# A hybrid decoder's mixer put into one order of steps for all engines: attention projections in pieces between the steps of the inversion

## The reference, cut to what matters

```python
for l in range(2):
    x = x + 0.5 * swiglu(rms_norm(x, ffn1_norm[l]), ...)
    h = rms_norm(x, mix_norm[l])
    dq, dk, dv, iq, ik, iw, gq, gk, gv, gz, ga, gb, mq = split_columns(h @ w_in[l])
    # A, 6 heads x 64: q and k normed per head; scores of the lightning indexer,
    #   sum_h iw_h * relu(iq_h . ik), 8 heads x 32; the 128 best keys of each query are kept,
    #   then softmax attention with a relative bias over them
    # B, 6 heads x 64: gated delta rule in chunks of 64 on silu(conv4(gq, gk, gv));
    #   needs the inverse of a unit lower triangle for each chunk; rms_norm, times silu(gz)
    # C, 4 heads x 64: attention of mq over 256 memory tokens, keys and values rms_norm(mem) @ w_mem_kv
    x = x + concat(A, B, C) @ w_out[l]
    x = x + 0.5 * swiglu(rms_norm(x, ffn2_norm[l]), ...)
```

## Time and profile before

| | |
|---|---|
| median of 3 runs | 2494.97 us (2494.83 to 2496.26) |
| the profiled execution's own time | 2497.04 us |
| its span | 2495.3 us |
| PE, DVE, ACT, POOL busy | 2359.1, 1121.6, 747.8, 455.5 us |
| mean granted clock of PE | 0.946 |

### The profile page before, as it was taken

One profiled execution on the slowest core, in us unless ns is written; L12 is line 12 of the kernel. 1 busy time (PEld: TensorE's weight loads), 2 busy tenths in 40 slices (PEclk: granted clock), 3 DMA queues, 4 the chain that ended last, 5 costly groups with the idle time before them and its releaser, 6 DMA issues.

```text
span 2495.3 us, 33780 instructions
## 1 busy us (share of the span) xinstructions
PE 2359.1 (95%) x14076; PEld 1882.7 (75%) x14076; DVE 1121.6 (45%) x1504; ACT 747.8 (30%) x983; POOL 455.5 (18%) x352
## 2 busy tenths in 40 slices
PE   7999999998889899999999999999879988999999
PEld 5888886776666778888878888868756767788887
DVE  4444333788543244343343343357874433443322
ACT  3222223433442132222232222244243321322221
POOL 4111011222432211110111110112224322111100
PEclk9999999999887799999999999998988968999999
DMA  4222221211000122222222222212210002222222
GB/s 150 101 95 90 93 94 67 102 68 68 28 2 1 68 81 88 101 99 93 95 85 101 101 84 99 100 41 99 85 62 17 2 1 84 85 86 99 97 93 80
DMA packets 28044, 192.32 MB, mean 77 GB/s; under 512 B 3104, under 2 KB 3232, under 8 KB 8992
## 3 DMA queue, kind: packets, MB, share of 16 engines
q1 hardware_dynamic: 27648, 189.80, 22.0%
q10 hardware_dynamic: 288, 0.94, 0.1%
HBM read 188.64 MB, written 2.10 MB: 76 GB/s over the span
## 4 chain that ended last, share of the span: by engine, by line
PE 84%; DVE 7%; issue 5%; POOL 2%; ACT 2%; DMA 0%; SPq 0%; POOLq 0%; ACTq 0%
PE psum L653 24%; PE psum L654 23%; PE psum L655 23%; PE psum L991 2%; PE psum L979 2%; PE psum L779 1%; DVE wl L1366 1%; PE psum L762 1%; DVE wrk L1449 1%; PE psum L965 1%; PE psum L858 1%; DVE gqT L1467 1%; POOL BT L584 1%; DVE m L1447 1%; PE psum L903 1%
## 5 line engine op out<-in xcount | busy, mean ns | idle before, releaser
L653 PE MATMUL psum<-XH,wh 128*128 128x512 f32 x1920 | 768.1, 400 | 53.0 <-DVE XL L1378 18.2
L654 PE MATMUL psum<-XL,wh 128*128 128x512 f32 x1920 | 754.5, 393 | 0.0
L655 PE MATMUL psum<-XH,wl 128*128 128x512 f32 x1920 | 753.9, 393 | 0.0
L653 PEld LDWEIGHTS psum<-XH,wh 128*128 128x128 f32 x1920 | 364.2, 190 | 146.7 <-issue 38.3
L654 PEld LDWEIGHTS psum<-XL,wh 128*128 128x128 f32 x1920 | 364.0, 190 | 81.5 <-issue 5.9
L655 PEld LDWEIGHTS psum<-XH,wl 128*128 128x128 f32 x1920 | 363.4, 189 | 79.0
L1066 ACT ACTIVATE wh<-raw 128x2048 fp32r<-128x2048 f32 x86 | 164.5, 1913 | 545.7 <-PE psum L655 545.4
L1366 DVE TENSOR_TENSOR wl<-raw,wh 128x2048 fp32r<-128x2048 f32 (+1 forms) x86 | 184.3, 2143 | 269.8 <-ACT wh L1066 269.8
L653 PE MATMUL psum<-HH,wh 128*128 128x512 f32 x704 | 278.1, 395 | 0.0
L655 PE MATMUL psum<-HH,wl 128*128 128x512 f32 x704 | 278.1, 395 | 0.0
L654 PE MATMUL psum<-HL,wh 128*128 128x512 f32 x704 | 278.1, 395 | 0.0
(11 more groups left out here) (241 smaller groups left out, 2429.0 us busy)
## 6 DMA issues: line engine op xcount, KB each, us to landing
raw<-weights SPq DMA_DIRECT2D x144, 1024.0 KB, 4.9
raw<-weights SPq DMA_DIRECT2D x32, 896.0 KB, 4.6
strips<-strip_table SPq DMA_DIRECT2D x2, 1536.0 KB, 6.6
xT<-xt SPq DMA_DIRECT2D x4, 512.0 KB, 9.3
memT<-memt SPq DMA_DIRECT2D x2, 1024.0 KB, 5.1
out<-xT SPq DMA_DIRECT2D x8, 256.0 KB, 6.0
cst<-masks ACTq DMA_DIRECT2D x1, 835.5 KB, 8.3
colsb<-cols ACTq DMA_DIRECT2D x1, 85.0 KB, 5.4
```

Source lines behind the costliest of these rows:

```text
L653: pe.matmul(out_ap, a_hi, b_hi, start=first, stop=False)
L654: pe.matmul(out_ap, a_hi, b_lo, start=False, stop=False)
L655: return pe.matmul(out_ap, a_lo, b_hi, start=False, stop=last)
```

## The change

All engines now walk one list, `MIX_ORDER`, which `_order()` writes. The units and groups stand in another order: iq, ik, sm, mk, mv, the twelve g groups, then dq, dk, va, mq, vb. The last five are cut into pieces of the eight slices and laid behind the steps of the set-up and of the inversion (`pull`); all are through behind the step y of level 4 of the second half. The 44 slots come after `u`: four behind u, three behind each r1, two behind each r2.

Selection is dealt out in 15 rounds over the g groups and 33 over the inversion. The index scores are six batches of four heads; each head keeps its own 32 rows of iqT and of ikT (which holds the key four times over), and writes its own psum bank. `ikz` is gone. The first tap of conv (`tap`) is done by ACT instead of DVE, the copies of transposed gv by ACT instead of DVE. LO_DVE is 1, so POOL splits seven of eight slices. POOL makes BT two levels ahead. The memory tokens are loaded at the start of the mixer, in SP's queue ahead of unit 2, and squared and split between the first groups. SBUF is laid out anew so that XH and XL stay whole through the inversion.

```diff
-MIX_SRC = (["iq", (O_DQ, 256), "small", (O_DQ + 256, 256), (O_DQ + 512, 256), (O_DV, 256), (O_DV + 256, 128)]
-           + [(O_MQ, 256)] + ["mk", "mv"] + [(O_G + 256 * i, 256) for i in range(6)]
+MIX_SRC = (["iq", "small", "mk", "mv"] + [(O_G + 256 * i, 256) for i in range(6)]
+           + [(O_DQ, 256), (O_DQ + 256, 256), (O_DQ + 512, 256), (O_DV, 256), (O_MQ, 256), (O_DV + 256, 128)]
...
+def _order():
+    order = []
+    rounds = [(b, r) for b in range(1, NB) for r in range(TOPK // 8)]
+    def sel(n):
+        for _ in range(min(n, len(rounds))):
+            order.append(("sel",) + rounds.pop(0))
+    def mm(name, c):
+        order.append(("mm", GROUP_AT[name, c], 0, KD))
+    def ev(name, c):
+        order.append(("ev", GROUP_AT[name, c]))
+    def norm(kind, *which):
+        for w in which:
+            order.append((kind, NORMS.index(w)))
+    def put(*names):
+        for n in names:
+            order.append(n if isinstance(n, tuple) else (n,))
+    mm("iq", 0)
+    put("ss", "rr")
+    ev("iq", 0)
+    put("mem1")
+    mm("iq", 1)
+    ev("iq", 1)
+    put("mem2")
+    mm("ik", 0)
+    put("mem3")
+    ev("ik", 0)
+    put("mem4")
+    mm("sm", None)
+    ev("sm", None)
+    put("mem5")
+    mm("mk", 0)
+    put("smt")
+    ev("mk", 0)
+    norm("sq", ("mk", 0))
+    put(("idx", 0), "gate1")
+    mm("mk", 1)
+    ev("mk", 1)
+    norm("sq", ("mk", 1))
+    put(("idx", 1), "gate2")
+    mm("mv", 0)
+    ev("mv", 0)
+    put("gate3", ("idx", 2))
+    mm("mv", 1)
+    ev("mv", 1)
+    put("gate4", ("idx", 3))
+    gates = {0: "gate5", 1: "gate6", 2: "gate7"}
+    pairs = [[("gq", 0), ("gq", 1)], [("gq", 2), ("gk", 0)], [("gk", 1), ("gk", 2)]]
+    for n in range(12):
+        name, c = ("gq", "gk", "gv", "gz")[n // 3], n % 3
+        mm(name, c)
+        if n == 3:
+            norm("hs", ("mk", 0), ("mk", 1))
+            norm("rs", ("mk", 0), ("mk", 1))
+        ev(name, c)
+        if n < 9:
+            put(("tap", n), ("conv", n))
+        if n < 2:
+            put(("idx", 4 + n))
+        if n in gates:
+            put(gates[n])
+        if n == 4:
+            norm("ap", ("mk", 0), ("mk", 1))
+        if n == 7:
+            put("silu_qk")
+            norm("sq", *pairs[0])
+        if n in (8, 9, 10):
+            norm("hs", *pairs[n - 8])
+            norm("rs", *pairs[n - 8])
+            norm("ap", *pairs[n - 8])
+            if n < 10:
+                norm("sq", *pairs[n - 7])
+        if n >= 2:
+            sel(1 if n < 7 else 2)
+    fill = []
+    for name, c in ([("dq", c) for c in range(3)] + [("dk", c) for c in range(3)] + [("va", b) for b in range(NB)]
+                    + [("mq", c) for c in range(2)] + [("vb", b) for b in range(NB)]):
+        cost = {"va": 0.36, "vb": 0.33}.get(name, 0.68)
+        fill += [(name, c, k, cost) for k in range(KD)]
+    later = []
+    def pull(target):
+        now = [x for t, x in later if t <= 0]
+        later[:] = [(t - 1, x) for t, x in later if t > 0]
+        for x in now:
+            order.append(x)
+        while fill and target > 0:
+            name, c, k, cost = fill.pop(0)
+            gi = GROUP_AT[name, c]
+            if order[-1][0:2] == ("mm", gi):
+                order[-1] = ("mm", gi, order[-1][2], k + 1)
+            else:
+                order.append(("mm", gi, k, k + 1))
+            target -= cost
+            if k == KD - 1:
+                order.append(("ev", gi))
+                if (name, c) in NORMS:
+                    nj = NORMS.index((name, c))
+                    later.extend([(0, ("sq", nj)), (1, ("hs", nj)), (1, ("rs", nj)), (2, ("ap", nj))])
+    put("silu_vz")
+    pull(5.4)
+    put(("vt", 0), ("vt", 1))
+    while order[-1][0] != "mm":
+        pull(1.3)
+    put(("vt", 2), ("vt", 3))
+    left = sum(x[3] for x in fill) - 9 * 0.7
+    for i, step in enumerate(INVERSION):
+        order.append(step)
+        pull(0.68 if i < 9 else left / 25)
+        if i >= 9:
+            sel(2 if step[0] == "x" else 1)
+    while fill or later:
+        pull(5.4)
+    put("ready")
+    slots = iter(range(N_SLOTS))
+    for step in RECURRENCE:
+        order.append(step)
+        for _ in range({"r1": 3, "r2": 2, "u": 4}.get(step[0], 0)):
+            n = next(slots, None)
+            if n is not None:
+                order.append(("att", n))
+        sel(1 if step[0] in ("u", "r1", "r2") else 0)
+    for n in slots:
+        order.append(("att", n))
+    assert not rounds
+    return order
...
                     for v in range(U_MIX, U_MIX + MIX_UNITS):
+                        if v == U_MIX + 2:
+                            sp.wait_ge(S["dn_done"], KD * (3 * L + 1))
+                            sp.dma_start(memT[:, :, :], memt).then_inc(S["mem_in"], 16)
...
-                        if v == U_MIX + 4:
-                            sp.wait_ge(S["sc_done"], 24)
-                            sp.wait_ge(S["acc_done"], 24)
-                            sp.dma_start(memT[:, :, :], memt).then_inc(S["mem_in"], 16)
...
-LO_DVE = 3
+LO_DVE = 1
...
+                        elif kind in ("kq", "y"):
+                            if kind == "kq":
+                                ahead = [(at_[0], 0)] if at_[0] < 2 else [(at_[0] - 2, 1)]
+                            else:
+                                g, j = at_
+                                ahead = [(b, j + 2) for b in (2 * g, 2 * g + 1) if j + 2 < LEVELS]
+                                ahead += [(b + 2, j + 2 - LEVELS) for b in (0, 1) if g == 0 and j + 2 >= LEVELS]
+                            for b, j in ahead:
...
+                    for step in MIX_ORDER:
+                        if step[0] == "ev":
+                            split_rest(step[1])
+                        elif step[0] == "att":
+                            combine(step[1] + 2)
+                        else:
+                            gdn(*step)
...
+                    def index_scores(batch):
+                        b, h0 = 1 + batch // 2, 4 * (batch % 2)
+                        wait_copied(GROUP_AT["ik", 0])
+                        if batch == 0:
+                            pe.wait_ge(S["mem_r"], 1)
+                        for i in range(4):
+                            n = 4 * batch + i
+                            if batch:
+                                pe.wait_ge(S["relu_done"], n - 3)
+                            r = slice(D_I * i, D_I * (i + 1))
+                            pe.matmul(bank[4 + i][:, 0:P * (b + 1)], iqT[r, h0 // 4, b * P:(b + 1) * P],
+                                      ikT[r, 0:P * (b + 1)], start=True, stop=True).then_inc(S["sc_done"], 1)
...
+                    def tap(n):
+                        dst = (gqT, gkT, gvT)[n // 3][:, n % 3, :]
+                        wait_copied(FIRST_CONV + n)
+                        act.activation(dst, cv[n % 2][:, 0:T], ACT.Copy, scale=convws[:, L, 0, n:n + 1]
+                                       ).then_inc(S["tap_done"], 1)
...
+                        dst = (gqT, gkT, gvT)[n // 3][:, n % 3, :]
+                        src = cv[n % 2]
+                        dve.wait_ge(S["tap_done"], of("tap_done", n + 1))
+                        for i in range(1, CONV):
+                            if i > 1:
                                 chain.join()
...
+                    for step in MIX_ORDER:
+                        kind, *at_ = step
+                        if kind == "ev":
+                            gi, = at_
+                            if copied(gi)[0] == "ev_dve":
+                                evac(gi)
+                            u = GROUPS[gi]["unit"]
+                            if LAST_OF_UNIT[u] == gi:
+                                split_lo(U0 + u + 2, LO_DVE)
+                        elif kind == "ap":
```

More of the change, by code:

```diff
@@ L148 @@
 JOB_HEAD = [H_A + _i for _i in range(H_M)] + list(range(H_A))
[L149 to L153, removed]
+N_SLOTS = N_JOBS + 4
+IDX_BATCHES = 6
+def _order():
[122 more added lines that the diff above has]
+    return order
@@ new lines, in small_step @@
+                    def small_step(kind):
+                        if kind == "ss":
+                            sum_squares(1)
+                        elif kind == "smt":
+                            wait_copied(GROUP_AT["sm"])
+                            pe.wait_ge(S["r_done"], 3 * L + 2)
+                            for c in range(NB):
+                                mm = pe.transpose(bank[2][:, c * SM:(c + 1) * SM],
+                                                  smT[:, c * P:(c + 1) * P], const("ident")[0:SM, 0:SM])
+                            mm.then_inc(S["sm_t"], 1)
+                        elif kind == "mem3":
+                            pe.wait_ge(S["mem_s"], 1)
+                            pe.matmul(bank[6][:, 0:NM], const("ones"), nsqm[:, :], start=True, stop=True)
+                            for m in range(2):
+                                mm = pe.matmul(bank[7][:, m:m + 1], nsqm[:, m * P:(m + 1) * P], one,
```

(33 more changed lines are left out.)

608 lines of the change are left out of this document (275 added, 333 removed).

## The result

The changed kernel takes 2547.4 us (median of 4 runs, 2541.4 to 2550.5), the kernel before 2494.9 beside it (2492.3 to 2496.3): 1.0209 times as long, 95% interval 1.0186 to 1.0231. It is slower, by 52.5 us where 46 were forecast. The profiled execution took 2549.8 us with a span of 2548.0.

A forecast was written before the change was run, and what follows sets the result against it. Only PE was taken to bound the mixer, by waiting and by running at 1.2 GHz. Its stages, 126 + 150 + 191 = 467 us against 443.8, gave +23 a layer, +46 in all: 2541 us, range 2460 to 2590.

The forecast's parts named there:

- Stage 3: Recurrence with all 44 slots: 116 us at full clock, 197 at 1.2 GHz; 191 taken.
- PEclk at 0.5 from there to the output projection: Sign of being right: low clock from the last w, about 670 us, to the output projection.
- Rival 1: Clock holds or soon returns in the recurrence with slots: 116 us there, 2391 in all; chance 0.11.
- Recurrence steps: r1 and r2 among the slots at 1.2 GHz: 7 x 3.1 and 7 x 2.9 us.
- The break-even: Change wins once recurrence with slots takes under 168 us, a third of it at full clock, earlier stages as forecast.
- Stage 1: From 394.5 us to the last gz group: PE work 112 plus waits and clock 14, 126 us.
- I take 14 of waits and clock (5 to 30): PE's waits and low clock up to the last gz group, from blocked or delayed DVE work: 14 us.
- mem5's wait: mk waits for mem5 on DVE, behind sm's evacuation and the next unit's split: 3 to 4 us.
- Stage 2: dq0 to the last w, projections among inversion steps: PE work 131 plus waits 19, 150 us (139 to 170).
- The last w: End of the inversion in the first layer, expected at about 670 us as a sign of being right.
- rival 3: DVE and POOL block each other more: waits of 33 us a layer become 55, 2585 in all; chance 0.07.
- Announced signs: POOL splits near 4.7 us, STT operations beside them 3 to 4, L779 under 9, PE idle under 35 a layer.

The follow-up runs named there:

- e7_kick2: Changed kernel plus 20 unread 128 x 512 matmuls a layer behind u's waits and two ahead of each slot's logits: 2489.2 us, 0.9988 of the kernel before.
- e10_best: Changed kernel with mem5 earlier, nine selection rounds moved into the set-up, and unread 128 x 512 matmuls mostly in PE's waits: 2431.8 us, 0.9751 of the kernel before.
- e2_rows32: Changed kernel plus two unread 512-column matmuls on 32 rows ahead of each slot's logits, 80 a layer: 2637.2 us, 1.0571 of the kernel before.
- e4_mem5: Changed kernel with the memory tokens' low part (mem5) made on DVE before sm's evacuation: 2532.7 us, 1.0144 of the kernel before.
- e1_dense: Changed kernel plus two unread 128 x 512 matmuls ahead of each slot's logits, 80 a layer: 2541.0 us, 1.0181 of the kernel before.

## Why the prediction was right, and where it was not

- **Stage 3 at 1.2 GHz decides the sign.** Right, and shown from both sides: with the clock held for most of stage 3 the change costs nothing (e7_kick2), with it held throughout and mem5 moved it wins (e10_best), and 80 matmuls more a layer on 32 rows change nothing at the clock and cost their full time (e2_rows32). "PEclk at 0.5 from there to the output projection": 167.2 of 179.8 us in each layer.
- **Rival 1's price.** 116 us at full was the forecast, 112 is the estimate from e7_kick2's second layer. At 0.50 I had 191 and it took 179.8. Recurrence steps were sized well (L1054 and L1060 together 21.6 us, forecast 7 x 3.1); the slots were sized 128.5 and took 118.5 to 851.7, and 10.2 us near the end ran at full, where I had taken off 6. Adding rows also counts overlap twice: from 688 to 851.7 the groups of PE add up to 172.8 us, while PE is busy 155.3.
- **The break-even.** Stage 3 under 168 was to win. With it at 160.9 and 137.5 (e7_kick2) the kernel is level with before, because the two stages ahead of it had been forecast 17.7 us too short; the break-even in the first layer was 150 (443.8 - 142.0 - 151.7).
- **Stage 1.** This is the step that failed in size: 126 forecast, 142.0 measured. The work was right: 123.8 us busy at a mean clock of 0.89 is 110 at full, forecast 112 (index scores 6.4, forecast 7). The term "I take 14 of waits and clock (5 to 30)" came out at 18.2 of waits and 13.6 of clock, 31.8, just outside its own bounds. mem5's wait, "3 to 4 us", was 6.65, because ML's eight operations met a POOL split (3.66 of its 6.95 us), and I had added no low clock beside any wait: it was down from 421.7 to 428.5 at this one, 493.4 to 500.2 and 510.4 to 517.3 at the next two. e4_mem5 took the first pair away and gained 7 us a layer, twice the wait that I had named.
- **Stage 2.** 150 forecast, 151.7 measured; 138.3 busy at 0.94 is 130 at full, forecast 131. Waits 13.4 and clock 8.3 against 19.
- **The last w.** 688.2, not 670: stage 1's 16 us and 2 of stage 2, just short of rival 3's 690. Its cause, DVE and POOL in each other's way, is real in ML and the masks. LO_DVE = 3 changes nothing in all, but by a shorter front and a longer stage 3; whether POOL's share of the splits is a lever stays open.
- **Announced signs.** POOL's split 4.26 us on the mean (4.7 announced), three taps of a conv on DVE 5.84 us beside it and 2.33 without (3 to 4 us for one blocked operation announced), L913 6.4 us (under 9), PE idle 46.7 us a layer (under 35 announced: wrong).
- **Right partly by offset.** 16 us too few in stage 1 and 11 too many in stage 3 make the sum look better than its terms; that they cancel is luck.

What stays open: which matmuls exactly hold the clock, and by how much e10_best's extra ones could be thinned out; its parts were not run one by one. Projections of real use in stage 3 in place of the extra matmuls (gz isn't needed before it) weren't tried, since the activations' buffers are written over there.

## What to carry to other kernels

When steps are rearranged, look at what is left alone at the end: the list here gave the inversion its dense cover and left 180 us a layer in which nothing lifts TensorE's clock. Price each stage at both clocks before moving work out of it, and count the low clock that comes with a wait of some us, too. Where no real dense work can be laid in, full-size matmuls that nobody reads can be, put mostly where PE waits anyway: some 134 of them in each stage 3 of e10_best cost 19 us a layer (130.8 against the estimated 112) and saved 68 (180 against 112).

## What was not expected of the hardware

- PE busy 204.0 of 211.5 us and the clock at 0.50 throughout (e2_rows32). The Trainium skill ("TensorE: Matmul & The Clock Gate", Part 1) has activity release the throttle and says that the clock follows how busy PE is; here busy time alone didn't do it, and the same matmuls on 128 rows did (e1_dense from 797.3, e7_kick2).
- The same work can go on at either clock. Block 3's last seven slots with logits, two extra matmuls in each, ran at 0.50 in the first layer of e7_kick2's profiled run and at 1.00 in its second; from the first of these logits to the output projection it is 60.3 us and 37.7.
- Two extra 128 x 512 matmuls a slot cost 1.15 us at 1.2 GHz, 0.57 each, more than the 0.43 that twice the projections' rate gives.
